# Attention by pairs of heads: fp32r scores on alternating row halves, values on alternating column halves

## The reference

```python
px = modulate(rmsnorm(x), ...) @ w_mix_in        # 512 tokens
pc = modulate(rmsnorm(ctx), ...) @ w_mix_in      # 256 context tokens
q, k, v, gb, gc, u = split_heads(px, ...)        # 8 heads of q, 2 of k and v, width 64, rmsnorm on q and k
qc, kc, vc, ... = split_heads(pc, ...)
q, k = apply_rope(q), apply_rope(k)
s = q @ concat([kc, k]).T * 64 ** -0.5           # 512 x 768 for each of the 8 heads
p = softmax(s)
a = p @ concat([vc, v])                          # 512 x 64 for each head
sc = gb * short_conv3(gc * u, conv_w)            # 512 channels
x = x + m5 * (concat([rmsnorm(a), rmsnorm(sc)]) @ w_mix_out)
```

## Time and profile before

| | us |
|---|---|
| three executions | 2873.36, 2872.82, 2866.63 |
| median | 2872.82 |
| span of the profiled execution | 2863.3 |
| PE busy in it | 2792.1 (98%) |
| DVE, ACT, POOL busy | 1489.5 (52%), 1141.4 (40%), 515.0 (18%) |
| QKV stage, about 661 to 715 | 54 |
| attention stage, 715 to 901 | 186 |

### The profile page before, as it was taken

One profiled execution on the slowest core, in us unless ns is written; L12 is line 12 of the kernel. 1 busy time (PEld: TensorE's weight loads), 2 busy tenths in 40 slices (PEclk: granted clock), 3 DMA queues, 4 the chain that ended last, 5 costly groups with the idle time before them and its releaser, 6 DMA issues.

```text
span 2863.3 us, 37055 instructions
## 1 busy us (share of the span) xinstructions
PE 2792.1 (98%) x14453; PEld 2234.9 (78%) x14453; DVE 1489.5 (52%) x2096; ACT 1141.4 (40%) x1699; POOL 515.0 (18%) x297
## 2 busy tenths in 40 slices
PE   8999999999999999998899999998999999999999
PEld 4888888866656688887888888887868877788887
DVE  6734434257546633335754656554367765653443
ACT  4221212224444432223655555554476663432221
POOL 0000000023111100002444434344332223100000
PEclk9999999999999999999999999999999999999999
DMA  6422323143102333322211212111211112332232
GB/s 234 154 75 87 115 67 107 53 142 117 37 30 91 124 96 90 95 93 99 79 53 45 65 55 62 51 52 45 67 67 60 60 53 99 96 103 91 94 97 81
DMA packets 69871, 241.77 MB, mean 84 GB/s; under 512 B 8218, under 2 KB 8346, under 8 KB 69314
## 3 DMA queue, kind: packets, MB, share of 16 engines
q1 hardware_dynamic: 62032, 221.28, 24.1%
q10 hardware_dynamic: 7666, 18.13, 1.9%
HBM read 232.74 MB, written 6.64 MB: 84 GB/s over the span
## 4 chain that ended last, share of the span: by engine, by line
PE 87%; ACT 6%; DVE 5%; issue 1%; DMA 1%; POOL 0%; ACTq 0%; DVEq 0%; SPq 0%; POOLq 0%
PE ps L1091 61%; PE ps L1475 3%; PE ps L1281 2%; PE ps L1576 2%; PE ps L1250 2%; PE ps L1372 2%; PE ps L1412 1%; PE ps L1268 1%; PE ps L1121 1%; PE ps L1302 1%; PE ps L1404 1%; ACT w_hi L456 1%; ACT r L456 1%; DVE f_t L474 1%; PE ps L1259 1%
## 5 line engine op out<-in xcount | busy, mean ns | idle before, releaser
L1091 PE MATMUL ps<-Nh,w_hi 128*128 128x512 f32 (+1 forms) x1808 | 660.8, 366 | 12.6 <-DVE Nl L463 6.2
L1091 PE MATMUL ps<-Nl,w_hi 128*128 128x512 f32 (+1 forms) x1808 | 630.9, 349 | 0.0
L1091 PE MATMUL ps<-Nh,w_lo 128*128 128x512 f32 (+1 forms) x1808 | 629.1, 348 | 0.0
L456 ACT ACTIVATE w_hi<-w_raw 128x1024 fp32r<-128x1024 f32 (+1 forms) x352 | 368.1, 1046 | 637.9 <-PE ps L1091 523.7
L463 POOL TENSOR_TENSOR w_lo<-w_raw,w_hi 128x1024 fp32r<-128x1024 f32 x125 | 308.8, 2470 | 750.3 <-ACT w_hi L456 746.3
L463 DVE TENSOR_TENSOR w_lo<-w_raw,w_hi 128x1024 fp32r<-128x1024 f32 (+1 forms) x227 | 281.8, 1241 | 257.0 <-ACT w_hi L456 247.3
L1091 PEld LDWEIGHTS ps<-Nh,w_hi 128*128 128x128 f32 x1808 | 343.3, 190 | 83.2 <-issue 33.3
L1091 PEld LDWEIGHTS ps<-Nl,w_hi 128*128 128x128 f32 x1808 | 343.6, 190 | 50.3 <-issue 5.6
L1091 PEld LDWEIGHTS ps<-Nh,w_lo 128*128 128x128 f32 x1808 | 343.4, 190 | 44.0
L1091 PE MATMUL ps<-x1h,w_hi 128*128 128x512 f32 (+1 forms) x784 | 272.2, 347 | 3.5 <-DVE x1l L474 1.8
L1091 PE MATMUL ps<-x1l,w_hi 128*128 128x512 f32 (+1 forms) x784 | 266.6, 340 | 0.0
(11 more groups left out here) (350 smaller groups left out, 4730.6 us busy)
## 6 DMA issues: line engine op xcount, KB each, us to landing
w_raw<-in_w_in SPq DMA_DIRECT2D x132, 512.0 KB, 3.5
w_raw<-in_w_proj SPq DMA_DIRECT2D x89, 512.0 KB, 3.5
w_raw<-in_w_ada SPq DMA_DIRECT2D x52, 512.0 KB, 4.2
w_raw<-in_w_out SPq DMA_DIRECT2D x48, 448.0 KB, 3.3
w_raw<-in_w_out SPq DMA_DIRECT2D x24, 512.0 KB, 3.5
w_raw<-in_w_mix_in SPq DMA_DIRECT2D x19, 512.0 KB, 3.5
w_raw<-in_w_bdn SPq DMA_DIRECT2D x16, 512.0 KB, 3.5
w_raw<-in_w_mix_out SPq DMA_DIRECT2D x8, 512.0 KB, 3.5
```

Source lines behind the costliest of these rows:

```text
L456: self.then_inc(self.e.activation(out, in_, func, **kw), sem)
L1091: ins = e.matmul(out[:, 512 * j:512 * j + n], a[:, kk, :], x[:, kk, c0:c0 + n], start=k == 0 and p == 0, stop=k == nt - 1 and p == 2)
```

## The change

The scores are computed for two heads at a time. Their heads lie on rows 0 to 63 and 64 to 127, and each of three fp32r passes (high by high, high by low, low by high) is issued first for one head, then for the other. For this q and k get a rounded copy (`rounded`, on ACT, fp32r) and a remainder (`remainder`, on POOL), while `rotated` now writes back to its scratch tile. The values are computed block by block: `vp` has no zeros any more and is 64 wide, and twelve fp32 matmuls of 128 columns alternate between output partitions 0 to 63 and 64 to 127. There are 16 steps m = 0 to 15 instead of 32 blocks, each with two softmax blocks and six tiles, in a new order. `turned(n)` stands at its own event again, and both `attend` of a pair stand at the event `score`. The conditions of some semaphores follow; four semaphores are merged into others, and the waits on them count accordingly.

```diff
 def attention_order():
-    out = []
+
+
+    out = [("score", 0)]
     fills = products("w_mix_in", [7 + i for i in range(12)])
-    for n in range(-1, 33):
-        if n + 1 < 32:
-            out.append(("score", n + 1))
-        h = n // 4 - 1
-        values = [("value", h, n % 4)] if n >= 4 and n % 4 < 3 else []
-        if 0 <= n < 32:
-
-            tiles = fills[3 * n - (n == 3):3 * n + 3 - (n == 2)]
-            if n == 0:
-                out += tiles[0:2] + [("vturn", 0)] + tiles[2:] + [("turn", n)]
-            elif n % 8 == 5:
-                out += tiles[0:1] + values + tiles[1:2] + [("turn", n)] + tiles[2:]
-            else:
-                out += [("vturn", 1)] if n == 2 else values
-                out += tiles[0:2 + (n == 3)] + [("turn", n)] + tiles[2 + (n == 3):]
+    for m in range(16):
+        tiles, n = fills[6 * m:6 * m + 6], 2 * m
+        score = [("score", m + 1)] if m < 15 else []
+        if m == 0:
+            out += tiles[0:2] + [("vturn", 0)] + tiles[2:4] + [("vturn", 1)]
+            out += [("turn", 0)] + tiles[4:5] + [("turn", 1)] + score + tiles[5:] + [("value", 0)]
+        elif m < 15:
+            out += [("turn", n)] + tiles[0:1] + [("turn", n + 1)] + tiles[1:2] + score + tiles[2:4]
+            out += [("value", m)] + tiles[4:]
         else:
-            out += values
-        if n in (12, 20, 28):
-            out.append(("square", "mixc", n // 8 - 1))
-        elif n in (14, 22, 30):
-            out.append(("square", "att", n // 8 - 1))
-    return out + [("value", 7, 1), ("value", 7, 2)]
+            out += [("turn", n)] + tiles[0:2] + [("turn", n + 1)] + tiles[2:] + [("value", m)]
+        if m in (6, 10, 14):
+            out.append(("square", "mixc", m // 4 - 1))
+        elif m in (7, 11):
+            out.append(("square", "att", m // 4 - 1))
+        if m == 14:
+            out.append(("square", "att", 2))
+    return out
...
-        self.qT = mem.put("qT", [P, 4, TX])
-        self.kT = mem.put("kT", [P, 2, T1])
-        self.vp = mem.put("vp", [P, 6, 4, P])
+        self.qTh, self.qTl = mem.put("qTh", [P, 4, TX], F32R), mem.put("qTl", [P, 4, TX], F32R)
+        self.kTh, self.kTl = mem.put("kTh", [P, 2, T1], F32R), mem.put("kTl", [P, 2, T1], F32R)
+        self.vp = mem.put("vp", [P, 6, 2, 64])
+        mixer = mem.at + 4 * T1
...
-        self.PT = [mem.put(f"PT{i}", [P, 6, TX]) for i in range(2)]
+        self.PT = [mem.put(f"PT{i}", [P, 6, P]) for i in range(4)]
...
-                r.use(ev, s.exp, ev[1] + 1)
+                for n in (2 * ev[1], 2 * ev[1] + 1):
+                    r.use(("score", n), s.exp, n + 1)
...
         elif ev[0] == "score":
-            n = ev[1]
-            h, qb = divmod(n, 4)
-            r0 = 64 * (h % 2)
-            w.wait_ge(s.q_out, 6 if h < 4 else 8)
-            out = pair(ps, bank_of(ev))
+            p, qb = divmod(ev[1], 4)
+            w.wait_ge(s.q_hi, 5 if p < 2 else 6)
+            w.wait_ge(s.q_lo, 5 if p < 2 else 6)
+            outs = [pair(ps, bank_of(("score", 2 * ev[1] + x))) for x in range(2)]
             for c0, nn in COLS1:
-                ins = e.matmul(out[:, c0:c0 + nn], t.qT[r0:r0 + 64, h // 2, qb * P:(qb + 1) * P],
-                               t.kT[r0:r0 + 64, h // 4, c0:c0 + nn], start=True, stop=True)
-            w.then_inc(ins, s.score)
+                for i, (qt, kt) in enumerate(((t.qTh, t.kTh), (t.qTh, t.kTl), (t.qTl, t.kTh))):
+                    for x in range(2):
+                        rows = slice(64 * x, 64 * x + 64)
+                        ins = e.matmul(outs[x][:, c0:c0 + nn], qt[rows, p, qb * P:(qb + 1) * P],
+                                       kt[rows, p // 2, c0:c0 + nn], start=i == 0, stop=i == 2)
+                        if c0 and i == 2:
+                            w.then_inc(ins, s.score)
         elif ev[0] == "turn":
             n = ev[1]
             out = pair(ps, bank_of(ev))
-            w.wait_ge(s.softmax, 4 * n + 4)
+            w.wait_ge(s.softmax, 8 * (n // 2) + 2 * (n % 2) + 6)
             for i in range(6):
                 c0 = i * P if i < 3 else 512 + (i - 3) * P
                 ins = e.transpose(out[:, c0:c0 + P], t.pr[n % 2][:, i * P:(i + 1) * P], cs("ident"))
             w.then_inc(ins, s.turned)
         elif ev[0] == "value":
-            _, h, piece = ev
-            w.wait_ge(s.pt, 8 * h + 8)
-            w.wait_ge(s.v_out, 8)
-            if h and h % 2 == 0:
-                w.wait_ge(s.att, h // 2)
-            for i in (2 * piece, 2 * piece + 1):
-                ins = e.matmul(ps[:, 6, :], t.vp[:, i, 2 * (h // 4) + h % 2, :], t.PT[h % 2][:, i, :],
-                               start=h % 2 == 0 and i == 0, stop=h % 2 == 1 and i == 5)
-            if piece == 2:
-                w.then_inc(ins, s.value)
+            m = ev[1]
+            p, qb = divmod(m, 4)
+            w.wait_ge(s.pt, 4 * m + 4)
+            w.wait_ge(s.v_out, 4)
+            if qb == 0:
+                w.wait_ge(s.att, p)
+            for i in range(6):
+                for x in range(2):
+                    ins = e.matmul(ps[64 * x:64 * x + 64, 6, qb * P:(qb + 1) * P], t.vp[:, i, p // 2, :],
+                                   t.PT[(2 * m + x) % 4][:, i, :], start=i == 0, stop=i == 5)
+            w.then_inc(ins, s.value)
...
+    def rounded(i):
+
+        w.wait_ge(s.q_out, i + 1 if i < 4 else 2 * i - 2)
+        dst = t.qTh[:, i, :] if i < 4 else t.kTh[:, i - 4, :]
+        w.copy(dst, t.qk[i % 2][1][:, 0:TX if i < 4 else T1], s.q_hi)
...
+            if i > 1:
+                rounded(i - 2)
...
     def turned(n):
-        h, qb = divmod(n, 4)
         src = pair(ps, B.of["turn", n][0]).rearrange("p (a b) -> p a b", a=2)[:, :, 0:384] \
             .rearrange("p a (b c) -> p a b c", c=P)
-        dst = t.PT[h % 2][:, :, qb * P:(qb + 1) * P].rearrange("p (a b) c -> p a b c", a=2)
+        dst = t.PT[n % 4][:].rearrange("p (a b) c -> p a b c", a=2)
         w.wait_ge(s.turned, n + 1)
-        w.wait_ge(s.value, max(h - 1, 0))
+        w.wait_ge(s.value, max(n // 2 - 1, 0))
...
-    due = None
     for ev in ATTENTION:
-        if due is not None and ev[0] != "mm":
-            turned(due)
-            due = None
-        if ev == ("score", 0):
-            attend(0)
+        if ev[0] == "score":
+            attend(2 * ev[1])
+            attend(2 * ev[1] + 1)
         elif ev[0] == "mm" and ev[3] == 0:
             if ev[2] > 7 and (ev[2] - 8) % 3 < 2:
                 conv_in(ev[2] - 8)
             highs(split_of("w_mix_in", ev[2]) - 1, last)
         elif ev[0] == "turn":
-            if ev[1] + 1 < 32:
-                attend(ev[1] + 1)
+            turned(ev[1])
+            if ev[1] == 5:
+                rounded(5)
             if 28 <= ev[1] < 31:
                 mixed_hi(ev[1] - 28)
-            due = ev[1]
...
     def rotated(i):
         raw, v, tt, y = (a[:] for a in t.qk[i % 2][0:4])
-        dst = t.qT[:, i, :] if i < 4 else t.kT[:, i - 4, :]
         w.wait_ge(s.q_cos, i + 1)
         w.tt(v[:, 0:TX], v[:, 0:TX], tt[:, 0:TX], ALU.add, s.q_n)
-        w.tt(dst[:, 0:TX], v[:, 0:TX], y[:, 0:TX], ALU.mult, s.q_out)
+        w.tt(v[:, 0:TX], v[:, 0:TX], y[:, 0:TX], ALU.mult, s.q_out)
         if i >= 4:
-            w.tt(dst[:, TX:T1], raw[:, TX:T1], y[:, TX:T1], ALU.mult, s.q_out)
+            w.tt(v[:, TX:T1], raw[:, TX:T1], y[:, TX:T1], ALU.mult, s.q_out)
...
     def values(half):
 
-        w.wait_ge(s.zeros, 2)
         w.wait_ge(s.v_turn, half + 1)
         src = pair(ps, B.of["vturn", half][0])[:, 0:384].rearrange("p (a b) -> p a b", b=P)
         for g in range(2):
-            for par in range(2):
-                w.ts(t.vp[:, 3 * half:3 * half + 3, 2 * g + par, 64 * par:64 * par + 64],
-                     src[:, :, 64 * g:64 * g + 64], 1.0, None, ALU.mult, None, s.v_out)
+            w.ts(t.vp[:, 3 * half:3 * half + 3, g, :], src[:, :, 64 * g:64 * g + 64], 1.0, None, ALU.mult, None, s.v_out)
...
     for ev in ATTENTION:
         if ev[0] == "score":
-            largest(ev[1])
-            if ev[1] == 0:
-                divided(0)
-            elif ev[1] == 2:
-                values(0)
-            elif ev[1] == 4:
-
+            for n in (2 * ev[1], 2 * ev[1] + 1):
+                largest(n)
+            for n in (2 * ev[1], 2 * ev[1] + 1):
+                divided(n)
+            if ev[1] == 2:
                 rotated(5)
-        elif ev[0] == "vturn" and ev[1] == 1:
-            values(1)
+        elif ev[0] == "vturn":
+            values(ev[1])
         elif ev[0] == "mm" and ev[3] == 0 and ev[2] > 7 and (ev[2] - 8) % 3 == 2:
             convolved((ev[2] - 8) // 3)
-        elif ev[0] == "turn" and ev[1] + 1 < 32:
-            divided(ev[1] + 1)
-            if ev[1] >= 28:
+        elif ev[0] == "turn":
+            if 28 <= ev[1] < 31:
                 mixed_lo(ev[1] - 28)
             if ev[1] == 30:
                 lows(split_of("w_mix_out", 0) - 2, last)
-        elif ev[0] == "value" and ev[1] % 2 == 1 and ev[2] == 2:
```

(55 more changed lines are left out.)

3 lines of the change are left out of this document (1 added, 2 removed).

## The result

The changed kernel takes 2882.54 us (median of 5 runs, 2880.97 to 2884.53), the kernel before 2871.79 on the same chip (5 runs, 2865.93 to 2873.36). The ratio is 1.0042, with a 95% interval of 1.0027 to 1.0057. It is slower by 0.4%, just over the bound under which I called a difference no change. 2871 was forecast, with a range of 2855 to 2893, "same" as the likeliest outcome and a chance of 0.32 for slower. The time lies in the wide range, 0.5 above the 2860 to 2882 that I gave my own case; the direction was not the one that I held for likeliest.

What follows compares the result with a forecast made beforehand. The prediction took PE as the bound (87% of the chain). Attention stage -20.8, QKV stage +13.4 and clock +6.0 gave -1.4 us: 2871 against a median of 2872.8, range 2855 to 2893.

Steps and rivals of the forecast that it cites:

- my own case: Scores and values both overlap and both kinds of wait come: 2871, own range 2860 to 2882, chance 0.48.
- Scores and values: Attention stage on PE: overlapped halves, 1.25 a score pair and 1.55 a value step before switches, save 46.1 us together.
- The rivals without overlap: Attention stage: nothing overlaps, 2893, chance 0.17; or only scores or only values overlap, 2879 to 2885, chance 0.13.
- the packing rule: Scores and values: each pair in the time of one, 1.05 and 1.22, 2865; counted inside the forecast's main case.
- The QKV loop: QKV stage: ACT's rounding waits for DVE's `rotated`, closing a loop through POOL of 10.7 us per unit of q.
- The step that made `kTl` the last thing before score 0: End of QKV stage: score 0 waits for POOL's remainder of k until 726.1, 11.1 us late.
- The 2.3 that I had added for a late `largest(0)`: Start of attention: DVE, still busy with the second k, delays the first maximum by 2.3, making 13.4 in all.
- The waits in the stage: New PE waits in the attention stage, mostly from queue order on ACT and DVE: 25.3 us in sum.
- the tail: End of attention stage: DVE's three low parts and the convolution make the fourth row tile late by 1.7.
- The clock: Six PE stretches of 4 to 6 us without work lower the clock, 1.0 each: 6 us.
- the 9.5 that I carried over: Whole kernel: the median of the runs lies 9.5 above the profiled span, added to the forecast span.
- the rival by which only one of them overlaps: Attention stage: scores alone overlap, +7, or values alone, +12; 2879 to 2885, chance 0.13.

Runs made afterwards that it cites:

- same_rows: The changed kernel with both heads' score matmuls on rows 0 to 63, leaving out the second head's scores: 2898.43 us in one run.
- serial: The changed kernel with score passes issued head by head and value matmuls column half by column half, not alternating: 2891.49 us.
- round_late: The changed kernel with ACT's rounding one step later, behind the next unit's exponential, and POOL's cosine ahead of the remainder: 2872.31 us.
- act_only: The changed kernel with ACT's rounding moved behind the next unit's exponential, POOL's order left as it was: 2873.46 us.
- banked: The changed kernel with rounding, cosine and `conv_in` moved, and score 1 in the V unit's bank, not that of unit 5's rotation: 2838.98 us.

## Why the prediction was wrong, and where it was right

- **Scores and values.** Right, to 0.01 a pair and within 0.1 a step. PE's work in the stage, 139.9 by the forecast (186 less 46.1), accounts for the stage with the waits and the clock below. The rivals without overlap are out. same_rows and serial show what these would have cost a step: 1.05 more for a pair of scores, 0.9 for a value step. By the packing rule of the Trainium skill (TensorE: Matmul & The Clock Gate, Part 3: Packing small matmuls) I had estimated 1.05 for a pair and 1.22 for a step; the trace has 1.24 and about 1.5, between that and no overlap.
- **The QKV loop.** Right in mechanism and period (10.5 against 10.7), and round_late and act_only show two parts of it, 1.05 and 0.75 of the 3.0 by which a unit grew; the other 1.2 was not taken apart. The remainder of k came within 0.8 of its forecast time.
- **A wait missed: the second bank.** The step that made `kTl` the last thing before score 0 was wrong. A pair's score needs two pairs of banks at once, and the second was read by DVE's sine of unit 5, which ended at 730.47, 3.5 behind `kTl`. Score 0 was 14.1 late and not 11.1. banked shows the cause, in the version with the other edits: 4.06 of wait became 1.10. The bank edit alone was not run on the changed kernel. The 2.3 that I had added for a late `largest(0)` was that same DVE work, put at the wrong place: the score itself waited for it, and the maximum then followed at once. Net 0.7.
- **The waits in the stage.** 27.9 without the tail, against 23.6: `gb` 17.2 (16.6 forecast), `gc` 6.3 (4.0), `cu` 2.4 (called no change from some 0.3 each), and 2.0 for `vp` and `pr` (3.0). Short by 4.3.
- **The clock: the term that was mis-sized.** I took 6 us, "since dense matmuls follow at once and not every gap need lower it". The four behind scores and the one before score 0 all lowered it; the sixth, before `vturn`, was only 1.0 long and did not (1.00 from 736 to 740). The stage is 180.4 = 139.9 of work + 27.9 of waits + 12.6. The 139.9 is the forecast's own figure, so the 12.6 is a remainder; the trace's spacings bear it out. 9.2 or 9.3 is the price of the four `gb` gaps as measured. Behind the 9.15 before score 0 the first pair took 2.2 and not 1.24, and the first two tiles 2.4 and not about 1.5: some 2. Near the end, behind a wait of 2.56 that I had not counted among the gaps, a turn took 1.13 and not 0.57 and two tiles 2.3 and not about 1.5: 1.4. My own bound from the earlier trace rows was 1.6 to 4.5 a gap; a value inside it, 2.1 for each of the six, would have given the 12.6.
- **The sum.** Forecast -1.4, traced +9.9. The miss of 11.3 is 6.6 (clock) + 3.0 (bank) + 4.3 (waits) - 2.3 (the maximum) - 0.3 (tail). So the step that failed above all is the price of the clock, 1.0 a gap in place of the 2.3 measured, then the waits of the stage, then the second bank. The median came 11 above the forecast (2882.5 against 2871.4). The median of before stayed at its place, so this is no matter of the 9.5 that I carried over, though only 2.2 of that is a fixed distance and the rest was which execution had been profiled.
- **The range and the rivals.** That the time lies in the wide range is luck: its upper end stood for no overlap at all, and both overlaps came. The time even falls into the 2879 to 2885 of the rival by which only one of them overlaps; the traces rule that rival out, and the time alone would have pointed to it. The chance of slower adds up to 0.31 from its own terms and not to 0.32.

## What to carry to other kernels

A gap on TensorE costs more than its length: here 4.3 us of idling cost 2.3 more at half clock, on average over four. Before calling an order good, look at what the step before the next matmul stands behind on its own engine: here four `conv_in` of 0.6 us, each queued behind two exponentials it had no need of, ate over half of what the change saved on PE (26.5 of some 46). When work is paired, each resource is needed twice at once; ask for the releaser of the second one too.
